# Norm behind an output projection: squares added by VectorE, u scaled in column chunks inside the next stage, a transposing stage folded in

## The reference, cut to what matters

```
h = h + concat(y_a, y_b) @ w_out
u = h * rsqrt(mean(h * h) + 1e-6) * norm_ffn
q = u @ w_query                       # 8 heads, 2 halves of 128
s1, s2 = q[half 0] @ sub_keys[0].T, q[half 1] @ sub_keys[1].T
v1, i1 = top_k(s1, 16);  v2, i2 = top_k(s2, 16)
top_s, pos = top_k(v1[:, None] + v2[None, :], 16)
experts = i1[pos // 16] * 128 + i2[pos % 16];  gate = softmax(top_s)
h = h + sum_k gelu(expert_u[experts] . u) * gate * expert_v[experts]
y = h * rsqrt(mean(h * h) + 1e-6) * norm_final
```

## Time and profile before

| | |
|---|---|
| median of 3 runs | 4279.36 us (4277.87 to 4286.69) |
| profiled execution | 4278.28 us |
| its span | 4276.7 us |
| PE busy | 3743.9 us (88%) |
| VectorE busy | 3242.4 us (76%) |
| ACT busy | 1204.4 us (28%) |
| POOL (GpSimd) busy | 1241.3 us (29%) |

### The profile page before, as it was taken

One profiled execution on the slowest core, in us unless ns is written; L12 is line 12 of the kernel. 1 busy time (PEld: TensorE's weight loads), 2 busy tenths in 40 slices (PEclk: granted clock), 3 DMA queues, 4 the chain that ended last, 5 costly groups with the idle time before them and its releaser, 6 DMA issues. The chain is left out here.

```text
span 4276.7 us, 66020 instructions
## 1 busy us (share of the span) xinstructions
PE 3743.9 (88%) x22546; PEld 3450.8 (81%) x22546; DVE 3242.4 (76%) x6415; ACT 1204.4 (28%) x2213; POOL 1241.3 (29%) x1054
## 2 busy tenths in 40 slices
PE   7998666999895868774769999999999999999997
PEld 6998554777785845443759999999999999999997
DVE  4431564666764248997977999999999999999998
ACT  3211232232322102215972222222222222222221
POOL 0211000000000000000004555556555555555563
PEclk8999566899998889887989999999999999999998
DMA  3775211000001100010458888888888888888885
GB/s 93 85 80 75 82 59 62 24 12 20 11 9 62 67 23 27 29 39 42 201 228 299 291 293 300 292 300 287 300 289 299 289 300 291 298 294 287 305 289 190
DMA packets 292099, 729.43 MB, mean 171 GB/s; under 512 B 27528, under 2 KB 138840, under 8 KB 290448
## 3 DMA queue, kind: packets, MB, share of 16 engines
q0 software_dynamic: 120560, 431.42, 32.6%
q1 hardware_dynamic: 171424, 296.57, 20.7%
HBM read 650.20 MB, written 77.70 MB: 170 GB/s over the span
## 5 line engine op out<-in xcount | busy, mean ns | idle before, releaser
L2512 POOL DMA_INDIRECT experts_u_row<-in_up_rows,experts_u_at x384 | 562.5, 1465 | 648.1 <-DVE experts_dot L2698 530.2
L107 PE MATMUL experts_up_ps<-experts_u_hi,experts_up_hi 128*128 128x352 f32 x2048 | 662.4, 323 | 26.8 <-DVE experts_u_lo L2674 24.7
L107 PE MATMUL experts_down_ps<-experts_act_hi,experts_down_hi 128*128 128x352 f32 x2048 | 675.4, 330 | 8.2 <-DVE experts_down_lo L2674 6.4
L108 PE MATMUL experts_down_ps<-experts_act_lo,experts_down_hi 128*128 128x352 f32 x2048 | 661.6, 323 | 0.0
L108 PE MATMUL experts_up_ps<-experts_u_lo,experts_up_hi 128*128 128x352 f32 x2048 | 661.2, 323 | 0.0
L109 PE MATMUL experts_up_ps<-experts_u_hi,experts_up_lo 128*128 128x352 f32 x2048 | 661.0, 323 | 0.0
L109 PE MATMUL experts_down_ps<-experts_act_hi,experts_down_lo 128*128 128x352 f32 x2048 | 660.9, 323 | 0.0
L2519 POOL DMA_INDIRECT experts_v_row<-in_down,experts_v_at x384 | 506.3, 1318 | 222.4 <-issue 112.8
L2698 DVE CUSTOM_DVE_ANT_0 experts_u_row<-experts_u_row,stream_u_rows_of 128x1024 f32<-128x1024 f32 x384 | 466.5, 1215 | 71.8 <-DMA experts_u_row<-in_up_rows,experts_u_at 68.8
L2711 DVE SCALAR_TENSOR_TENSOR stream_h_rows_of<-experts_v_row,experts_weight,stream_h_rows_of 128x1024 f32<-128x1024 f32 x384 | 496.0, 1292 | 14.2 <-DVE experts_weight L2703 6.8
L2717 DVE TENSOR_TENSOR stream_h<-stream_h,experts_down_ps 128x704 f32<-128x704 f32 x512 | 450.4, 880 | 68.0 <-PE experts_down_ps L109 67.1
(11 more groups left out here) (380 smaller groups left out, 6626.5 us busy)
## 6 DMA issues: line engine op xcount, KB each, us to landing
experts_up<-in_up SPq DMA_DIRECT2D x128, 512.0 KB
experts_down<-in_down SPq DMA_DIRECT2D x128, 512.0 KB
gates<-spread_spread SPq DMA_DIRECT2D x11, 4096.0 KB
experts_gates<-gates SPq DMA_DIRECT2D x64, 704.0 KB
cols<-inp_done POOLq DMA_DIRECT2D x27, 576.0 KB
inp_w_in<-in_w_in SPq DMA_DIRECT2D x27, 512.0 KB
pick_w_query<-in_w_query SPq DMA_DIRECT2D x16, 512.0 KB, 4.0
experts_u_row<-in_up_rows,experts_u_at POOLq DMA_INDIRECT x384
```

The lines of the kernel that those rows point to most:

```text
L107: pe.matmul(out, w_hi, x_hi, start=start, stop=False)
L108: pe.matmul(out, w_hi, x_lo, start=False, stop=False)
L2512: pool.indirect_dma_start(u_row[b][:], None, up_rows_d, bass.IndirectOffsetOnAxis(ap=u_at[slot][:, b, a:a + 1], axis=0)).then_inc(u_row_lo ...
```

## The change

Five edits in the four functions, with these new pieces:

- `output_projection`: ahead of VectorE's three adds of the last tile, it adds the squares of tiles 1 to 6 into those of tile 0 (L1884 in the new file, `joined`). PE then multiplies ones with two tiles instead of eight: the joined one and the last (L1842, L1845). ACT's square of the first 704 columns of a tile no longer waits for the add of the last 384. VectorE writes mean + eps bank by bank into `mean_square`, which outlives the stage (L1896). Root, reciprocal and scaling leave the stage, and so does the load of norm_ffn.
- `pick_experts`: ACT takes the root in the three chunks of the queries (L2042), VectorE the reciprocal of a chunk and then scales u in that chunk (L2097, L2103), and PE's queries wait for each tile of a chunk (`u_ready`). The 37 memsets go to POOL. SP loads norm_ffn first, and `eye` and `iota` after the last keys.
- The transposes of `turn_rows` follow on PE and ACT behind their last head, in seven of the picking's banks, and VectorE's two instructions behind its last head. `turn_rows` as a stage is gone.
- `spread_gates` uses the `eye` and `iota` that are there.

```diff
 def output_projection(nc, h, h_rest, u, mean_square, x_kept_d, y_d, w_out_d):
@@ tensor
-                pe.wait_ge(h_ready, START + 3 * KD)
-                for k in range(KD):
-                    pe.wait_ge(squared, START + k + 1)
-                    for c, (lo, n) in enumerate(OUT_CHUNKS):
-                        mm = pe.matmul(out[0][c][:, 0:n], ones[:], u[:, k, lo:lo + n], start=(k == 0), stop=(k == KD - 1))
-                    mm.then_inc(sum_done, 1)
+                pe.wait_ge(joined, START + KD - 2)
+                pe.wait_ge(h_ready, START + 3 * (KD - 1))
+                for c, (lo, n) in enumerate(OUT_CHUNKS):
+                    pe.matmul(out[0][c][:, 0:n], ones[:], u[:, 0, lo:lo + n], start=True, stop=False)
+                pe.wait_ge(squared, START + KD)
+                for c, (lo, n) in enumerate(OUT_CHUNKS):
+                    pe.matmul(out[0][c][:, 0:n], ones[:], u[:, KD - 1, lo:lo + n], start=False, stop=True).then_inc(sum_done, 1)
@@ scalar
-                    act.wait_ge(h_ready, START + 3 * (k + 1))
+                    act.wait_ge(h_ready, START + 3 * k + 2)
                     act.activation(u[:, k, 0:DENSE], h[:, k, :], ACT.Square)
+                    act.wait_ge(h_ready, START + 3 * k + 3)
                     act.activation(u[:, k, DENSE:KEPT], h_rest[:, k, :], ACT.Square).then_inc(squared, 1)
-                act.wait_ge(rms_step, START + 1)
-                act.activation(inv_rms[:], inv_rms[:], ACT.Sqrt).then_inc(rooted, 1)
@@ vector
                 def add(q, s, m):
-                    if not (isinstance(m, int) and m == KD - 1):
+                    if isinstance(m, int) and m == KD - 1:
+                        for k in range(1, KD - 1):
+                            dve.wait_ge(squared, START + k + 1)
+                            if k > 1:
+                                dve.wait_ge(joined, START + k - 1)
+                            dve.tensor_tensor(u[:, 0, :], u[:, 0, :], u[:, k, :], ALU.add).then_inc(joined, 1)
+                    else:
                         split_w(1 - s, m + 1)
...
-                dve.wait_ge(sum_done, START + KD)
-                inverse_rms_steps(dve, rooted, out[0], inv_rms, OUT_CHUNKS, D, rms_step, START)
-                for k in range(KD):
-                    dve.scalar_tensor_tensor(out=u[:, k, 0:DENSE], in0=h[:, k, :], scalar=norm_g[:, k:k + 1], in1=inv_rms[:, 0:DENSE],
-                                             op0=ALU.mult, op1=ALU.mult)
...
+                for c, (lo, n) in enumerate(OUT_CHUNKS):
+                    dve.wait_ge(sum_done, START + c + 1)
+                    dve.tensor_scalar(mean_square[:, lo:lo + n], out[0][c][:, 0:n], 1.0 / D, RMS_EPS, ALU.mult, ALU.add).then_inc(mean_ready, 1)

 def pick_experts(nc, h, h_rest, mean_square, u, u_d, picks, rows, eye, iota, norm_g_d, w_query_d, keys_d, eye_d, iota_d):
@@ sync
-                sp.dma_start(iota[:], iota_d).then_inc(iota_loaded, 16)
+                sp.dma_start(norm_g[:], norm_g_d).then_inc(g_loaded, 16)
...
+                sp.dma_start(eye[:], eye_d).then_inc(eye_loaded, 16)
+                sp.dma_start(iota[:], iota_d).then_inc(iota_loaded, 16)
@@ gpsimd
+                pool.memset(best[:], 0.0)
...
+                last.then_inc(zeroed, 1)
@@ tensor
                             for k in range(KD):
+                                if s == 0:
+                                    pe.wait_ge(u_ready, START + c * KD + k + 1)
                                 mm = pe.matmul(q_ps[at_q % 3][:, 0:n], w[s][:, k * P:k * P + P], u[:, k, lo:lo + n], start=(k == 0), stop=(k == KD - 1))
...
+                for i, (src, first, row, _, k0) in enumerate(TURNS):
+                    if i >= len(turn_banks):
+                        pe.wait_ge(turned_out, START + i - len(turn_banks) + 1)
+                    for k in range(QUAD):
+                        mm = pe.transpose(turn_banks[i % len(turn_banks)][:, k * P:k * P + P], src[:, k0 + k, first + row:first + row + P], eye[:])
+                    mm.then_inc(turned, 1)
@@ scalar
                 st.start(act, vec)
+                for lo, n in KEPT_CHUNKS:
+                    act.activation(mean_square[:, lo:lo + n], mean_square[:, lo:lo + n], ACT.Sqrt).then_inc(rooted, 1)
...
+                for i, (_, _, _, dst, _) in enumerate(TURNS):
+                    act.wait_ge(turned, START + i + 1)
+                    act.activation(dst, turn_banks[i % len(turn_banks)], ACT.Copy).then_inc(turned_out, 1)
                 place_keys(PEER_HEADS - 1)
@@ vector
-                dve.memset(best[:], 0.0)
...
+                inv_rms = mean_square
+                dve.wait_ge(g_loaded, START + 16)
+                for c, (lo, n) in enumerate(KEPT_CHUNKS):
+                    dve.wait_ge(rooted, START + c + 1)
+                    dve.reciprocal(inv_rms[:, lo:lo + n], inv_rms[:, lo:lo + n]).then_inc(inverted, 1)
+                    dve.wait_ge(inverted, START + c + 1)
+                    for k in range(KD):
+                        for src, first, end in ((h, lo, min(lo + n, DENSE)), (h_rest, max(lo, DENSE), lo + n)):
...
+                                last = dve.scalar_tensor_tensor(out=u[:, k, first:end], in0=src[:, k, first - base:end - base], scalar=norm_g[:, k:k + 1],
+                                                                in1=inv_rms[:, first:end], op0=ALU.mult, op1=ALU.mult)
+                        last.then_inc(u_ready, 1)
+                dve.wait_ge(zeroed, START + 1)
...
+                dve.scalar_tensor_tensor(out=rows.at[:], in0=picks[:, 1, tiles, :], scalar=float(N_KEYS), in1=picks[:, 0, tiles, :],
...
+                dve.tensor_copy(rows.gate[:], picks[:, 2, tiles, :]).then_inc(picks_listed, 1)

-def spread_gates(nc, picks, gates_d, eye_d, iota_d):
+def spread_gates(nc, picks, gates_d, eye, iota):
@@ sync
-                sp.dma_start(eye[:], eye_d).then_inc(consts_loaded, 16)
-                sp.dma_start(iota[:], iota_d).then_inc(consts_loaded, 16)
@@ tensor, vector
-                pe.wait_ge(consts_loaded, START + 32)
-                dve.wait_ge(consts_loaded, START + 32)
```

More of the change, by code:

```diff
@@ L1955, in pick_experts @@
         sums = sb("sums", [P, GROUP_TILES, 2, CANDIDATES])
+        turn_banks = [*q_ps, *s_ps]
+        QUAD = BANK // P
+        TURNS = [(src, first, b * P, dst[:, b, half * BANK:half * BANK + BANK], half * QUAD)
+                 for b in range(BLOCKS) for half in range(KD // QUAD) for src, first, dst in ((u, DENSE, rows.u), (h_rest, 0, rows.h))]
         with nc.Block() as block:
```

101 lines of the change are left out of this document (36 added, 65 removed).

## The result

The changed kernel takes 4240.4 us in the median of 4 runs (4231.92 to 4246.4). The kernel before, run beside it on the same chip, takes 4280.38 (4 runs). The ratio is 0.9903, with a 95% interval of 0.9882 to 0.9924: **faster by 1.0%**, and 5.4 us above the forecast of 4235, inside its range. The profiled execution took 4231.92 us. In a later set of runs the changed kernel took 4224.9 us against 4264.48, a ratio of 0.9902 (0.9877 to 0.9927).

A forecast was written before the change was run, and what follows sets the result against it. The prediction saw two seams where engines work one after another, 42.8 and 14.5 us, with VectorE leading the picking. -32.1 + 0.6 - 12.6 = -44.1 us from 4278.28 gave 4234.2, stated as 4235 us, range 4226 to 4246.

The forecast's parts named there:

- the first seam: Between the output projection and PE's first query: 32.1 us less, then 0.6 us more for semaphores ahead of the loads.
- the 1.6 us of margin: At the picking's start: the first scaled tile ready at 1520.4, 1.6 us ahead of PE's first query at 1522.0.
- The scaling at no cost: Inside the picking: VectorE's scaling makes it late by 0 to 3 us, taken up by 17.3 us of first-head waits.
- The second seam: Behind the picking, before PE turns picks: 12.6 us less, with the row transposes moved into idle time of PE.
- the end of the bounds that was taken: At the second seam: PE starts 0.1 to 1.9 us behind a barrier without a load; 0.1 was taken.
- The three zeros: In the picking, each priced at 0: memsets on POOL, a table load for the root, PE's waits for u.
- PE's waits for u: In the first two heads' queries: 48 waits, 0 to 3 us in all, taken as 0.
- The prediction's rival: VectorE's 12.1 us of waits at the picking's loop head change with the loop's place: 4223 to 4240 us; 8%.
- Thin cover: Rival: costs set at 0 (memsets, PE's waits) and a late PE start add up to 11 us, 4236 to 4246; 15%.
- PE's experts' loop: Rival: moved code makes PE's jump back in the experts' loop need a fetch, 31 rounds, some 4303 us; 3%.
- the picking was pulled forward: Rival denied this: something holds the picking's end, so only the second seam's gain remains, 4267 us; 4%.
- released by keys and not by VectorE: Sign of being right: PE's first query, at 1522, waits for the load of the keys, not for VectorE's scaled tile.

The follow-up runs named there:

- changed_again: The changed kernel itself, unaltered, run once more on another chip beside later variants; 4224.9 us, ratio 0.9902 to the kernel before.
- keys_waited_later: The changed kernel with PE's wait for the keys moved from ahead of the query to ahead of the first score products; 4225.99 us, ratio 0.9907 to the kernel before.
- constants_behind: The changed kernel with the 37 memsets on VectorE behind its scaling of u, none on POOL; 4229.22 us, ratio 0.9913 to the kernel before.

## Why the prediction was right

It put the time at 4235 us, by -32.1 + 0.6 at the first seam and -12.6 at the second.

- *The first seam* measured -31.33 against -31.5. Its parts: from the last bank's add to the end of mean + eps 4.22 us (4.25 foreseen); SP's loads of w_query 2.07 us behind that, 0.54 more than before (0.6); first scaled tile done at 1517.11, 6.5 us behind it (6.0). The query came 1.3 us later, which leaves the 1.6 us of margin nearly as worked out. Joins and ones were priced by the right rows: 8.27 us for six (7.9), 1.99 for each set of three ones (1.9).
- *The scaling at no cost.* VectorE came to its first head at 1534.47, 16.1 us behind the first query; its scores had been copied by 1533.91. It was 0.6 us late, within the 0 to 3 foreseen, and its waits in the first head fell from 17.3 to 16.9 us.
- *The second seam* measured -12.3 against -12.6. VectorE ends at 1931.77 and PE starts 1.12 us later: a barrier of 1.0 and 0.1, the end of the bounds that was taken.
- *The three zeros.* POOL's memsets: shown at nothing, above. They took 6.1 us and not 7.6, since one starts every 0.16 us though each is 0.21 long. The root: the three of a chunk each take 1.29 us together, with no load of a table before them. The rows show why. The last load ahead of them (1118.44) stands before a root too (L1096, of the RWKV heads), and between it and 1513.27 ACT runs only copies, squares and roots. The page ScalarE: Activation LUTs (Table sets: the hidden batching unit) in the Trainium skill asks for a switch only where the function is not in the set that is loaded, so by it none was due here, and the prediction's 2.66 us read too much into it. Nor does a switch cost that much in this trace: from the end of ACT's last exponential, through the load, to the start of that earlier root it is 1.4 us (1118.43 to 1119.85). PE's waits for u: the pickings with them (410.9 and 412.0) stand beside three without (410.5, 409.4 and 411.2), 1.1 us more in the mean, which is also what two profiles of one kernel differ by; and the first scores were copied 15.5 us behind the first query, where it was 15.2 before. So they cost 0 to 1 us or so.
- *What the sum left out.* Seams, picking and spreading give -42.0 us where the forecast has -44.1. The 2.1 are 0.2 and 0.3 at the seams, and 1.6 behind them, of which 1.0 is in the waits at the loop's head (13.1 in place of 12.1). That is scatter: the same kernel waited 12.2 there in changed_again, and its picking took 410.9, 0.4 more than before. The prediction's rival had these waits move by -12.1 to +4.7 with the loop's place. The change did not move them by more than they scatter; they did move, by 2.7 to 3.7, where 37 instructions more stand ahead.
- *The rivals.* Thin cover did not come about, though the median of 4240.4 lies in its interval: two sets of runs gave 0.9903 and 0.9902, where the forecast stands for 0.9897, and the 5 us between are less than the scatter of the code ahead. That the median came so near to 4235 is in part luck; the seams, measured to a few tenths as forecast, are not. PE's experts' loop did not change (1984.83 us busy of 2016.70), and the picking was pulled forward in full.

The prediction named as a mark of the right account a first query "released by keys and not by VectorE". The first profile says VectorE; that it is the keys is shown by their landing 0.2 us ahead of the query, and by keys_waited_later, which took their wait away and had the query 1.3 to 1.75 us earlier.

## What to carry to other kernels

A seam in which the engines work one after the other is worth more than any of the stages around it: look for work that the engine with the next task can do while it would wait (the joins), move what needs no barrier behind the barrier, and let the consumer start on the first chunk. Before trusting a cost of nothing, name the cover and measure its width; here 17 us of waits in the first head took up the scaling, and in constants_behind 6 us of memsets as well. And read the small waits that no engine explains: three at the head of a loop of four rounds were worth 12 us, as much as the change won at the second seam, and went with three lines.

## What the runs showed that I had not expected

- Writing the loop out saved 15.1 us where its waits were 12.2. Of the rest, 1.4 us are small gaps between VectorE's instructions in the seven later heads (each 0.1 to 0.3 shorter), and 1.5 us lie in the first head, whose wait for spread keys was 1.7 us shorter. In the kernel before the same edit saved 13.7: the 12.1 of its waits, 1.3 of small gaps and 0.3 in the first head. So 13.5 or so is what the loop costs; the 1.5 was not seen again.
- Of the three jumps back the third is dear: 6.56, 5.55 and 6.08 us in three profiles of the same loop, beside 3.17 to 3.44 for the first two (before: 5.60 beside 3.28 and 3.19). With 37 instructions more ahead of the loop, in all, the three cost 4.3, 4.3 to 4.4 and 7.2 to 7.4. What sets these sizes stays open.
- The code ahead of the change, the same in all kernels up to the joins, came to the last bank's add anywhere in 21 us (1489.14 to 1510.15). A change worth less than 10 us cannot be read from the whole time of a few runs of this kernel; the stages of one profile each show it to about 1 us.
